# A hybrid decoder layer on one core: the forget gate in four column tiles, the residual's matmuls behind the transposes, and the two blocks of v on either side of the channel mean

## The reference

```
xn   = rmsnorm(x) * norm_mix_g
q, k, v, f_logit, glu_in = split(xn @ w_in)        # 512, 512, 512, 8, 1024 columns
log_f = log_sigmoid(f_logit + b_f)                 # 8 heads
att  = softmax(q k^T / 8 + c_t - c_s, causal) v    # c = cumsum(log_f) over tokens
a, g = split(glu_in + b_glu);  u = a * sigmoid(g)
conv = silu(layernorm(causal depthwise conv(u), width 31))    # 512 channels
h    = x + [att, conv] @ w_out
hn   = rmsnorm(h) * norm_ffn_g
gates = softmax over the top 4 of 32 of (hn @ w_router + b_router)
h   += sum over experts e of gates_e * (clamped SwiGLU(hn @ w_gu[e] + b_gu[e]) @ w_down[e] + b_down[e])
out  = rmsnorm(h) * norm_final_g
```

## Time and profile before

| | |
|---|---|
| median of 3 runs | 1076.37 us (1075.48 to 1077.9) |
| profiled execution, its own time | 1078.2 us |
| its span | 1076.5 us |
| busy in the span: PE, DVE, ACT, POOL | 90%, 23%, 13%, 3% |
| chain that ended last | DMA 48%, PE 42%, DVE 6%, ACT 1% |

### The profile page before, as it was taken

The page is one execution under the profiler, slowest core; times in us unless marked ns, Lnnn a source line. Parts: engine busy times, 40 slices in busy tenths (PEclk is TensorE's granted clock), DMA queues, the critical chain, the costliest instruction groups (busy, mean ns, idle before and its releaser), DMA issues.

```text
span 1076.5 us, 12696 instructions
## 1 busy us (share of the span) xinstructions
PE 968.6 (90%) x5670; PEld 401.2 (37%) x5671; DVE 246.1 (23%) x533; ACT 139.1 (13%) x263; POOL 35.4 (3%) x36
## 2 busy tenths in 40 slices
PE   9988979999999999998988888988988888889886
PEld 6864543333333333333333333323333333333232
DVE  2996451111111111111111111001111111110112
ACT  4224221000000000000000000000000000000002
POOL 4006020000000000000000000000000000000000
PEclk9998989999999999999999999999999999999999
DMA  9903959999999999999999999999999999999993
GB/s 303 385 16 120 430 236 379 429 427 427 427 427 428 427 428 426 428 427 427 427 427 426 427 427 427 428 428 428 428 427 428 428 427 427 427 427 426 427 426 136
DMA packets 39528, 422.00 MB, mean 392 GB/s; under 512 B 5313, under 2 KB 9457, under 8 KB 14896
## 3 DMA queue, kind: packets, MB, share of 16 engines
q1 hardware_dynamic: 37664, 420.84, 93.1%
q10 hardware_dynamic: 1808, 0.33, 0.2%
HBM read 420.09 MB, written 1.05 MB: 391 GB/s over the span
## 4 chain that ended last, share of the span: by engine, by line
DMA 48%; PE 42%; DVE 6%; ACT 1%; issue 1%; SPq 0%; another core or an unknown queue 0%; DVEq 0%; ACTq 0%
DMA ring<-in_w_gu 48%; PE work L978 35%; PE resid L978 5%; DVE main L909 2%; DVE main L906 1%; DVE main L902 1%; PE work L1286 1%; ACT main L611 1%; DMA ring<-in_w_dw 1%; DVE amax L753 0%; PE work L1093 0%; DVE main L788 0%; PE work L1175 0%; DVE top_i L845 0%
## 5 line engine op out<-in xcount | busy, mean ns | idle before, releaser
L978 PE MATMUL work<-ring,main 128*64 128x512 f32 (+1 forms) x3104 | 694.7, 594 | 59.6 <-DMA ring<-in_w_gu 57.8
L978 PEld LDWEIGHTS work<-ring,main 128*64 128x64 f32 (+1 forms) x3104 | 220.3, 137 | 509.2 <-issue 389.5
L902 DVE TENSOR_SCALAR main<-work 128x512 f32<-128x512 f32 x32 | 22.1, 691 | 752.1 <-PE work L978 752.1
L611 ACT ACTIVATE main<-main 128x512 f32<-128x512 f32 x32 | 20.2, 630 | 503.4 <-DVE main L902 503.4
L978 PE MATMUL resid<-main 128*128 128x512 f32 x136 | 71.2, 612 | 0.9 <-DVE main L962 0.9
L978 PE MATMUL work<-ring 128*128 128x256 f32 (+1 forms) x288 | 71.3, 410 | 0.0
L622 ACT ACTIVATE main<-work 64x512 f32<-64x512 f32 x63 | 37.2, 591 | 227.6 <-PE work L978 227.3
L978 PEld LDWEIGHTS work<-ring 128*128 128x128 f32 x288 | 55.2, 192 | 14.4 <-issue 7.8
L978 PEld LDWEIGHTS work<-select,main 128*128 128x128 bf16 x1584 | 49.1, 99 | 26.9 <-issue 26.9
L978 PE MATMUL work<-select,main 128*128 128x64 bf16 x1584 | 53.1, 195 | 0.9 <-DVE select L887 0.9
L730 DVE SCALAR_TENSOR_TENSOR main<-ring,dw_cols,main 128x256 f32<-128x256 f32 x116 | 46.5, 477 | 1.3 <-ACT main L491 1.1
(11 more groups left out here) (179 smaller groups left out, 276.3 us busy)
## 6 DMA issues: line engine op xcount, KB each, us to landing
ring<-in_w_gu SPq DMA_DIRECT2D x128, 2048.0 KB, 47.3
ring<-in_w_down SPq DMA_DIRECT2D x64, 2048.0 KB, 48.0
ring<-in_w_in SPq DMA_DIRECT2D x3, 2048.0 KB, 14.3
ring<-in_w_in SPq DMA_DIRECT2D x4, 1024.0 KB, 11.9
ring<-in_w_out SPq DMA_DIRECT2D x2, 2048.0 KB, 18.9
main<-in_x SPq DMA_DIRECT2D x2, 512.0 KB, 4.5
result<-main SPq DMA_DIRECT2D x4, 256.0 KB, 2.7
ring<-in_b_gu SPq DMA_DIRECT2D x12, 64.0 KB, 5.1
```

The lines of the kernel that those rows point to most:

```text
L611: nc.scalar.activation(sig_h, gate_h, ACT.Sigmoid, scale=SWIGLU_ALPHA).then_inc(sig_ready, 1)
L902: V.tensor_scalar(gate_h, work[:, GATE_BANK, :], SWIGLU_LIMIT, None, ALU.min).then_inc(gate_clamped, 1)
L978: return nc.tensor.matmul(out_, lhsT, rhs, start=start, stop=stop, skip_group_check=True)
```

## The change

1. The forget gate is computed in four column tiles. `wf_sb` gets 32 columns for each block of rows (8 of weights, the rest cleared by GpSimd first, for which ScalarE's load of it now waits), and block kb goes to output rows 32 (kb % 4) and up. ScalarE copies the 128 rows of partial sums to `f_parts` (`f_copied`), and a matmul with `f_sum`, made by VectorE from the identity, adds them (`add_f_parts`); it stands behind glu_a's first block. proj_done 1 is signalled there.
2. `start_with_x(0, ...)` moves from ahead of the transposes to ahead of the gate; `start_with_x(1, ...)`, with `x_added`, from ahead of the gate to behind the first glu block.
3. The transposes of w_dw move behind the gate, with a semaphore of their own (`taps_turned`), and ScalarE's copy to `dw_cols` behind its copy of the partial sums.
4. `values(10, ...)` is done whole before the mean; `values(11, ...)` moves from behind the second scores to between mean and variance. ScalarE's `copy_values(10)` moves ahead of the root.

```diff
--- before.py
+++ after.py
@@ -136,6 +136,8 @@
         dw_rows = unit(2)[0:TAPS, 3 * P:3 * P + D_CONV]
         bgu_raw = unit(3)
         fg = unit(16)[0:HEADS, 0:6 * SEQ].rearrange("p (n t) -> p n t", n=6)
+        f_parts = unit(15)[:, 7 * SEQ:8 * SEQ]
+        wf_sb = unit(16)[:, 7 * SEQ:8 * SEQ].rearrange("p (k h) -> p k h", k=KB)
         count_i = unit(16)[:, 6 * SEQ:7 * SEQ].bitcast(I32)
 
         v_sb = blocks(0, 2).rearrange("p (s n) -> p s n", s=TB)
@@ -171,7 +173,7 @@
         cols = sb("cols", [P, 36], F32)
         dw_cols = sb("dw_cols", [P, CB, TAPS], F32)
         G_MIX, B_A, B_G, B_DW, LN_G, LN_B, G_FFN = 0, 8, 12, 16, 20, 24, 28
-        wf_sb = sb("wf_sb", [P, KB, HEADS], F32)
+        f_sum = sb("f_sum", [P, HEADS], F32)
         bf_col = sb("bf_col", [HEADS, 1], F32)
         wr_sb = sb("wr_sb", [P, KB, E], F32)
         br_row = sb("br_row", [P, E], F32)
@@ -217,6 +219,7 @@
         vecs_turned, cols_ready, xn_turned, xnt_ready, x_added = sem("vecs_turned"), sem("cols_ready"), sem("xn_turned"), sem("xnt_ready"), sem("x_added")
 
 
+        wf_zeroed, f_sum_ready, f_done, f_copied, taps_turned = sem("wf_zeroed"), sem("f_sum_ready"), sem("f_done"), sem("f_copied"), sem("taps_turned")
         proj_done, proj_copied, u_ready = sem("proj_done"), sem("proj_copied"), sem("u_ready")
         taps_started, sum_cleared, tap_done, fg_step, decay_exp, decay_ready = sem("taps_started"), sem("sum_cleared"), sem("tap_done"), sem("fg_step"), sem("decay_exp"), sem("decay_ready")
         mean_done, centred, squared, squares_summed, var_done, var_ready, root_ready = sem("mean_done"), sem("centred"), sem("squared"), sem("squares_summed"), sem("var_done"), sem("var_ready"), sem("root_ready")
@@ -367,6 +370,7 @@
             pool.wait_ge(ident_step, 1)
             nc.gpsimd.affine_select(out=ident[:, :], in_=ident[:, :], compare_op=ALU.not_equal, fill=1.0,
                                     base=0, pattern=[[-1, P]], channel_multiplier=1).then_inc(ident_ready, 1)
+            nc.gpsimd.memset(wf_sb[:, :, :], 0.0).then_inc(wf_zeroed, 1)
             nc.gpsimd.memset(u_pad[:, :, 0:PAD], 0.0).then_inc(pads_ready, 1)
             nc.gpsimd.memset(mean_w[:, :], 1.0 / D_CONV).then_inc(consts_ready, 1)
             nc.gpsimd.memset(ones_b[:, :], 1.0).then_inc(consts_ready, 1)
@@ -445,7 +449,8 @@
 
         @block.scalar
         def _(act):
-            act.dma_start(wf_sb[:, :, :], w_in[:, F_COL:F_COL + HEADS].rearrange("(k p) n -> p k n", p=P)).then_inc(wf_in, 16)
+            act.wait_ge(wf_zeroed, 1)
+            act.dma_start(wf_sb[:, :, 0:HEADS], w_in[:, F_COL:F_COL + HEADS].rearrange("(k p) n -> p k n", p=P)).then_inc(wf_in, 16)
             act.dma_start(bf_col[:, :], b_f.rearrange("(a b) -> a b", b=1)).then_inc(bf_in, 16)
 
             def mean_square(src, junk, into, done):
@@ -461,11 +466,15 @@
                 nc.scalar.activation(stat[:, 4 + t:5 + t], stat[:, 2 + t:3 + t], ACT.Sqrt).then_inc(x_root, 1)
             act.wait_ge(vecs_turned, 1)
             nc.scalar.activation(cols[:, :], work[:, 3, 0:36], ACT.Copy).then_inc(cols_ready, 1)
-            nc.scalar.activation(dw_cols[:, :, :], work[:, 3, 64:64 + 32 * CB].rearrange("p (c j) -> p c j", c=CB)[:, :, 0:TAPS],
-                                 ACT.Copy).then_inc(cols_ready, 1)
             act.dma_start(wr_sb[:, :, :].rearrange("p (m b) n -> p m (b n)", b=2), w_router.rearrange("(m p b) n -> p m (b n)", p=P, b=2)).then_inc(router_in, 16)
             act.dma_start(br_row[:, :], b_router.partition_broadcast(P)).then_inc(router_in, 16)
 
+
+            act.wait_ge(f_done, 1)
+            nc.scalar.activation(f_parts, work[:, 0, 0:SEQ], ACT.Copy).then_inc(f_copied, 1)
+            act.wait_ge(taps_turned, 1)
+            nc.scalar.activation(dw_cols[:, :, :], work[:, 3, 0:32 * CB].rearrange("p (c j) -> p c j", c=CB)[:, :, 0:TAPS],
+                                 ACT.Copy).then_inc(cols_ready, 1)
 
             act.wait_ge(proj_done, 1)
             act.wait_ge(bf_in, 16)
@@ -541,9 +550,9 @@
 
             act.wait_ge(centred, 1)
             nc.scalar.activation(ln_tmp, conv_y, ACT.Square).then_inc(squared, 1)
+            copy_values(10)
             act.wait_ge(var_ready, 1)
             nc.scalar.activation(ln_s[:, 1, :], ln_s[:, 0, :], ACT.Sqrt).then_inc(root_ready, 1)
-            copy_values(10)
             act.wait_ge(normed, 1)
             for c in range(CB):
                 done = nc.scalar.activation(ln_tmp[:, c, :], conv_y[:, c, :], ACT.Sigmoid,
@@ -682,6 +691,8 @@
                 V.reciprocal(into, mid[1]).then_inc(scale_sem, 1)
                 dve.wait_ge(scale_sem, n + 1)
 
+            dve.wait_ge(ident_ready, 1)
+            V.tensor_reduce(f_sum[:, :], ident[:, :].rearrange("p (i h) -> p h i", i=4)[:, 0:HEADS, :], AX.X, ALU.add).then_inc(f_sum_ready, 1)
             for t in range(TB):
                 inv_rms(t, stat[:, t:t + 1], (stat[:, 2 + t:3 + t], stat[:, 4 + t:5 + t]), stat[:, 6 + t:7 + t],
                         x_squared, x_mean, x_root, x_scale)
@@ -997,23 +1008,16 @@
 
                 return mm(resid[:, t, h * HALF:(h + 1) * HALF], ident[:, :], x_sb[:, t, h * HALF:(h + 1) * HALF], True, False)
 
-            pe.wait_ge(x_in[0], 16)
-            start_with_x(0, 0)
-            start_with_x(0, 1)
             turn_normed(0)
             turn_normed(1)
 
             pe.wait_ge(vecs_in, 16 * 6)
             nc.tensor.transpose(work[:, 3, 0:28], vec_rows, ident[0:28, 0:28])
             for b in range(2):
-                nc.tensor.transpose(work[:, 3, G_FFN + b:G_FFN + KB:2], gain_rows[:, b:2 * P:2], ident[0:KB // 2, 0:KB // 2])
-            pe.wait_ge(dw_in, 16)
-            for c in range(CB):
-                last = nc.tensor.transpose(work[:, 3, 64 + 32 * c:64 + 32 * c + TAPS], dw_rows[:, c * P:(c + 1) * P],
-                                           ident[0:TAPS, 0:TAPS])
+                last = nc.tensor.transpose(work[:, 3, G_FFN + b:G_FFN + KB:2], gain_rows[:, b:2 * P:2], ident[0:KB // 2, 0:KB // 2])
             last.then_inc(vecs_turned, 1)
             turn_normed(2)
-            pe.wait_ge(cols_ready, 2)
+            pe.wait_ge(cols_ready, 1)
             turn_normed(3)
 
             def arrived(name):
@@ -1026,21 +1030,38 @@
                 return last
 
 
-            start_with_x(1, 0)
-            start_with_x(1, 1).then_inc(x_added, 1)
+            start_with_x(0, 0)
+            start_with_x(0, 1)
             pe.wait_ge(xnt_ready, 4)
             pe.wait_ge(wf_in, 16)
             for kb in range(KB):
-                last = mm(work[0:HEADS, 0, 0:SEQ], wf_sb[:, kb, :], xn_t[:, kb, :], kb == 0, kb == KB - 1)
-            last.then_inc(proj_done, 1)
-
+                i = kb % 4
+                last = mm(work[32 * i:32 * i + 32, 0, 0:SEQ], wf_sb[:, kb, :], xn_t[:, kb, :], kb < 4, kb >= 4)
+            last.then_inc(f_done, 1)
+            pe.wait_ge(dw_in, 16)
             for c in range(CB):
+                last = nc.tensor.transpose(work[:, 3, 32 * c:32 * c + TAPS], dw_rows[:, c * P:(c + 1) * P], ident[0:TAPS, 0:TAPS])
+            last.then_inc(taps_turned, 1)
+
+            def add_f_parts():
+                pe.wait_ge(f_sum_ready, 1)
+                pe.wait_ge(f_copied, 1)
+                mm(work[0:HEADS, 0, 0:SEQ], f_sum[:, :], f_parts, True, True).then_inc(proj_done, 1)
+
+            for c in range(CB):
+                if c == 1:
+                    start_with_x(1, 0)
+                    start_with_x(1, 1).then_inc(x_added, 1)
+                if c == 2:
+                    pe.wait_ge(cols_ready, 2)
                 if c == 3:
                     pe.wait_ge(proj_copied, 1)
                 for at, name in ((0, "glu_a"), (SEQ, "glu_g")):
                     if c % 2 == 0:
                         pe.wait_ge(glu_in[c // 2][name], 16)
                     last = columns(BANK_OF[2 + c], at, name, c)
+                    if (c, name) == (0, "glu_a"):
+                        add_f_parts()
                 last.then_inc(proj_done, 1)
 
             for n in range(6, 10):
@@ -1064,12 +1085,13 @@
 
             arrived("v")
             pe.wait_ge(proj_copied, 6)
-            values(10, range(0, 3))
+            values(10, range(KB)).then_inc(proj_done, 1)
             pe.wait_ge(consts_ready, 5)
             pe.wait_ge(tap_done, CB * OPS)
             pe.wait_ge(proj_copied, 7)
             channel_mean(MEAN_BANK).then_inc(mean_done, 1)
-            values(10, range(3, KB)).then_inc(proj_done, 1)
+            pe.wait_ge(proj_copied, 8)
+            values(11, range(KB)).then_inc(proj_done, 1)
 
 
             def scores(g):
@@ -1121,7 +1143,6 @@
             scores(0)
             pe.wait_ge(proj_copied, 10)
             scores(1)
-            values(11, range(KB)).then_inc(proj_done, 1)
             scores(2)
             turn(0)
 
```

## The result

The changed kernel took 1078.7 us (median of 11 runs), the kernel before 1076.37 (11 runs); one run of the changed kernel's 11, at 1138 us, came with a mean granted clock of 0.85 against 0.99 in the others and is not compared. The ratio is 1.0021 (95% interval 1.0013 to 1.0030): 2.3 us slower. The interval excludes no change, and the size is just above the 0.2% under which the prediction called a difference untellable. The forecast was 1077.5, in a range of 1075.0 to 1079.9.

A forecast was written before the change was run, and what follows sets the result against it. The first expert's start, behind the VectorE taps and the VectorE/GpSimd order up to the first transpose of probabilities, was to bound the kernel. That transpose 0.7 to 1.5 later, taken as 1.1: 1076.37 + 1.1 = 1077.5 us, range 1075.0 to 1079.9.

The forecast's parts named there:

- rival 2: Start: transposes may not wake TensorE's clock, which rises at 15.8 to 17.9; first transpose +2.7 to +3.5, 1079.5 us; chance 0.23.
- The end follows the first freed slot: Expert stream: the end is the first freed buffer's moment (165.15 before) plus an unchanged length, one for one.
- The transposes at 1.2 GHz, xn_t: Start: eight transposes take 1.8 us from 7.25; VectorE's passes over xn_t run 9.95 to 12.45, gain 0.65 us.
- The clock's rise: TensorE's start: the clock rises at 11.7 to 13.9, taken as 12.7, so x ends at 13.7.
- The gate in four tiles: Forget gate on TensorE: 1.1 us instead of 3.56, bounds 0.87 and 3.5; glu starts at 15.15 instead of 16.70.
- Rival 4: Forget gate: the column tiles don't run side by side, 2.4 us more before glu; +3.4, 1079.8 us; chance 0.05.
- The gate's sum and the memset: Gate's sum ends at S = 19.2; a GpSimd memset delays VectorE's L708, putting product u at 26.9, 0.7 later than before.
- Rival 1: The q_aug memset blocks nothing on VectorE: taps end at 78.15, first transpose +0.2 to -0.3, 1076.4 us; chance 0.25.
- Mean and variance: After the taps: mean like before or 0.1 later; variance at VectorE at 87.5 instead of 86.08, L781 at 90.2.
- The interleaving with GpSimd: VectorE against GpSimd's b_gu casts and subtractions: first transpose of probabilities at 102.7, or 101.9 in the old order; 1.1 later taken.
- From one execution to the median: Profiled execution before lies 1.8 us above the median; the same +1.1 us was added to the median 1076.37.
- Rival 3: Whole gain comes through: clock rises at 11.7, memset blocks nothing, first transpose 1.25 earlier, 1075.1 us; chance 0.06.

The follow-up runs named there:

- late clearing: Changed kernel, but GpSimd clears q_aug only after VectorE has made the decays: 1076.46 us, ratio 1.0003 against the kernel before.
- v's blocks undone: Changed kernel with part 4 undone, blocks 10 and 11 of v as in the kernel before: 1078.2 us, ratio 1.0018.
- the fastest version: Changed kernel, q_aug cleared after decays, 11 idle matmuls, v's old order, GpSimd's last b_gu subtraction behind the third maxima: 1069.6 us, ratio 0.9928.
- the earlier wait: Kernel before, with GpSimd's last subtraction and cast of b_gu only after VectorE has normalised the second probabilities: 1076.16 us, ratio 0.9998.
- the second profile of before: Kernel before run again without edit: median 1076.43 us, ratio 1.0003; its profiled execution took 1078.67 us.
- the idle matmuls: Changed kernel with 11 instead of 5 matmuls whose result nobody reads, ahead of the first transpose: 1076.0 us, ratio 0.9994.

## Why the prediction was right, and where its sizes were off

The time lies in the range, 1.2 us above the forecast, and on the side that the forecast named, though most of its chances (0.65) stood on no tellable change. Some of that is luck: 1078.7 is nearer to rival 2's 1079.5, whose mechanism did not happen, than to the forecast. By its steps:

**The end follows the first freed slot.** Held in fourteen profiles to within 1.7 us: 910.1 to 911.8 us from the one to the other.

**The transposes at 1.2 GHz, xn_t.** 9.77 to 12.25 against 9.95 to 12.45. The copy into cols was a little sooner.

**The clock's rise.** "11.7 to 13.9, I take 12.7". By the lengths of x's passes it was near 11.4 in the profile of the changed kernel, by 11.1 with late clearing, near 11.5 with v's blocks undone, near 12.6 and 13.2 in two others. So the range was 0.6 too late at its near end. Filling the rest ahead of the transposes took 2.7 us off the median, which shows that rest, which the change opened, as a large part of the loss in typical executions; the changed kernel's profile alone would not have shown it.

**The gate in four tiles.** 1.1 assumed, 1.07 measured. Rival 4 is out.

**The gate's sum and the memset.** The sum ended at 18.72. The first decay was expected at S + 5.43, the memset 0.1 ahead of it, and u at S + 7.65; measured S + 5.42, the memset 0.09 behind it, and S + 7.90. So the order was the other way round, and it was the second decay that waited. Rival 1 fell with the late clearing, which brought 1.9 us by the ratios and 2.2 by the medians. By the Trainium skill's rule on the shared port pair ("SBUF — State Buffer", "Who interferes with whom") a memset blocks too; the trace agrees, with 1.96 us for the instruction that began 0.12 us behind it.

**The taps' end.** 79.55 expected, 79.26 measured; the unbroken stretch from u is 52.64 in both.

**Mean and variance.** Variance on VectorE at 87.5 expected, 87.37 measured; L792 at 90.07 against 90.2. The prediction put the mean of the kernel before at 1.2 GHz; its 0.67 us and a granted clock of 1.00 from 78.8 to 79.9 say full speed, with 0.51 only behind it. The sum didn't use this.

**The interleaving with GpSimd.** "102.7, or 101.9 with the old order"; 101.90 came, but not with the old order, so that number is a coincidence. L792 did wait for the cast, and cast, L792, subtraction, L764 and cast followed each other as forecast. The taps ended 0.29 us early, and the steps behind them were each taken up to 0.2 too long: the subtraction ends 3.9 us behind L792, not 4.1, and the earlier trace rows already had the cast end 1.75 us behind L781 (91.98 against 90.23), where I read 1.9. Together that is the 0.8. The pauses of 3.58 and 3.31 us were real, and the runs show what they are worth: moving the subtraction out of the way brought 0.15% with v's blocks as changed, and together with v's old order 0.49% (0.9977 to 0.9928), two thirds of what the fastest version gains. In the kernel before, the earlier wait gave nothing in the median.

**The third scores.** Not in the forecast: they wait for the first exponentials, so with block 11 done early TensorE rests 8.2 us. It costs little while GpSimd holds VectorE back (0.1 to 0.6 us for part 4 by the ratios of three pairs, 0.2 to 1.0 by their medians, none clear of noise), and 0.34%, 3.6 us by the ratios, 3.1 by the medians, once it doesn't.

**From one execution to the median.** This is the term that was mis-sized: +1.1 us was added to a median as it stood. In the profiles the difference at the first transpose is 0.7 us (0.5 against the second profile of before), and the spans differ by -0.6. The medians differ by 2.3. The spans of all runs say how much of that is the choice of executions: their median is 1074.7 in the kernel before (33 runs on one chip, 27 on another) and 1076.7 in the changed one, so the profile of before was 1.8 us over its median and that of the changed kernel 0.8 under. The loss within the span is 2.0 us, and 0.24 lies outside it (own time less span is 1.75 on average before, 1.99 after). Where in a typical execution the 2.0 us arise is known only in part. In the five profiles of the new start with its five idle matmuls, x's passes took on average 0.3 us more than in the changed kernel's own; of the old start's four profiles the one used lies 0.15 later at u than their mean. That is 0.4 or so of the 1.3 between 0.7 at the first transpose and 2.0 in the span, from few executions. The rest stays open; what speaks for the start is that the idle matmuls gave the median 2.7 and their profile's u only 1.75.

**Rival 2**, a late rise because transposes don't wake the clock, did not happen: in all five profiles of the new start it rose by 13.2, and with late clearing behind transposes alone. The Trainium skill's statement in "TensorE: Matmul & The Clock Gate", section "Part 4: PE-mode transpose", that a transpose doesn't count as busy for the clock, isn't borne out by these float32 transposes (the section's own figures are for bf16): rows at 7.04, 9.36 and 11.06 above, read by their lengths. **Rival 3**, the full gain, fell with the memset.

## What to carry to other kernels

Before moving a step, list what its semaphore releases on engines that look idle: here a memset of 1.8 us took back about what four column tiles had gained (1.9 us each), and one added wait returned it. When VectorE shows an instruction several times its usual length, look at GpSimd's row that ends just before it does. And a gap that a reordering opens on TensorE ahead of critical work can cost more than itself, because the work behind it may run at half the clock; the profile of one execution can hide it, so compare several, and set the span of the one you read against the spans of all runs.

## What the runs showed that I had not expected

Rows of a two-operand VectorE instruction and a GpSimd subtraction overlap, but the work hardly does. In the changed kernel 92.60 - 91.66 = 0.94 us of L792 lies beside the subtraction, and that is 0.78 us longer than usual (4.85 against 4.07): that fits a row that begins at issue and then waits. With late clearing 1.03 us lie side by side and the subtraction is 0.87 longer. The other way round, an L793 that came during a subtraction ended 1.08 us behind it. A cast did the same: it held L792 to its own end (91.52; L792 then ran 1.08 us more). In all these rows whichever is under way holds the other, but for some 0.15 us.

Of two tensor_scalars in a row the first, 0.09 us ahead of the memset's start, ran in 0.28 us beside it, and the second, 0.12 behind its start, waited to its end, 1.7 us more. A tensor_tensor beside the same memset was not held (u, 0.43 us, with late clearing).

Four column tiles of 32 columns ran 16 float32 passes of 256 columns in 1.07 us, against 3.62 in one tile.
